# Four dense layers in exact fp32 on one core: first pieces and last pieces in halves, layer 1's small steps moved, and turned projections with one product for both halves of x

## The chip, the cores and the metric

One core of one Trainium2 chip. The metric is the device time of one execution in microseconds (us). The program holds all its work in one launch; its loops are unrolled when it is built.

## The reference, cut to what matters

x has 256 tokens of 2048 features and goes through four layers. Each is x + mix(rmsnorm(x) @ w_in) @ w_out, and a last rmsnorm follows:

```python
# layer 0: 8 heads of chunked attention with a relative bias, 4 heads of mLSTM       w_in 2048 x 9224
proj = rmsnorm(x, norm_g) @ w_in
y = concat(attention(qa, ka, va) * silu(za), sigmoid(ob) * mlstm(qb, kb, vb, gates) * silu(zb))
x = x + y @ w_out                                                                    # 2048 x 2048
# layer 1: RG-LRU behind a causal convolution, 8 heads of gated delta rule           w_in 2048 x 6160
# q, k, v: convolution, silu, l2norm of q and k; per head a 64-block triangular solve
# layer 2: 8 heads of a mixture of dilated windows, 4 heads of differential attention, rotary q and k
h = rmsnorm(x, norm_g) @ w_in                                                        # 2048 x 8192
yb = (softmax(q1 k1^T) - lam * softmax(q2 k2^T)) v
x = x + (concat(ya, yb) * silu(z)) @ w_out
# layer 3: 16 heads of causal attention, rotary q and k                              w_in 2048 x 8192
# out = rmsnorm(x) * final_norm
def _rope(t, pos):
    x1, x2 = split(t, 2, axis=-1)
    return t * cos + concat(-x2, x1) * sin
```

All is fp32.

## The kernel before, in words

**Products in three parts.** A product of fp32 matrices is made from fp32r parts: a = hi + lo, where hi is a copy in fp32r and lo what is left. ACC gets hi*hi + hi*lo + lo*hi. For x the parts are `XH` and `XL` (16 k-tiles of 128 features by 256 tokens), for a layer's output `YHA`, `YHB`, `YLA`, `YLB`; for the weights `WH` and `WL`.

**Jobs and pieces.** `job_list` (L77) names the projections in order; a job is 512 columns of a weight matrix (`few` jobs: 8 or 16). `piece_list` (L124) cuts each into pieces of 2 k-tiles x 512 columns (512 KB), 626 in all, and that order is the program's clock. For every piece SP issues a load into one of 8 `RAW` buffers (L600), ScalarE makes the high part (L985), VectorE the low one (L1330), and TensorE the products. `LOOK = 5`: the splits run five pieces ahead of the products; `WH` has 6 buffers. A load waits for the products eight pieces back.

**Two forms of product.** In "tok" form (L685 to 687) x is stationary and 512 columns of weights stream: 2 k-tiles x 2 token halves x 3 = 12 products per piece. In turned form ("feat", L692 to 694) 128 columns of weights are stationary and the 256 tokens stream: 2 x 4 x 3 = 24. Turned results stand feature by token, as scores need them. In layers 2 and 3 `q0`, `k0`, `q1`, `k1` are turned, two jobs each (b = 0, 1); the order there is q0 k0 v0 q1 k1 v1, then `zs`, `zg` and `out`.

**Accumulators.** Four PSUM banks `ACC0` to `ACC3`: job j uses two, and the first product of job j + 2 waits until job j is evacuated (L659 to 663). `evacuate` (L987 on ScalarE, L1332 on VectorE, L1821 on GpSimd) runs after a job's last piece. For a rotary job VectorE does, for each of two banks, one multiplication by cos (L1373) and two by sin on 64 partitions (L1377), and GpSimd adds them (L1849).

**The plan.** All other work is in small steps written out by hand. `put(slot, step, item, banks)` (L347) puts a step behind the products of piece `slot`; every engine walks the pieces and does its share of each step there (`go`), in order, so a step waits in its engine's queue behind all before it. PSUM banks `PM0` to `PM3` are dealt out in turn to steps that ask for them; a step waits until its bank was read (`read_out`). In `plan1` (L423), with b1 the first piece of layer 1: `norm_sum` (L845, 1200, 1622) sums the squares of q and k of four heads with 32 products of one column and takes two square roots; `delta_a`, `delta_k`, `delta_q` (L865 to 882) make the decayed products; `tri` (VectorE and ScalarE) inverts 16-blocks; `level_x` and `level_y` (L884, L900) join blocks at levels 4, 5 and 6, each using what ScalarE (L1242) or VectorE (L1697, L1701) made of the step before; `solve1` to `solve4`; `gate_lru`, `decay_lru`, `root_lru`, `scan` are the RG-LRU's. The functions of the scalar engine switch tables (ACT_TABLE_LOAD) between silu, square root, sigmoid and exponential.

**Start.** Transposed x lies in `Y` in six parts, and `x0` splits two k-tiles of it before each of the first eight pieces. `warm` (L697) issues 5 products on zeros before the first piece. A tile `VC` holds all per-partition vectors.

**End.** When the last job is added to x (L1362), ScalarE sums the last squares, `rms_a` makes 1/rms of both token halves, both engines scale what `gained` had multiplied by the final gain, and SP stores four times 512 columns of both halves (L637).

Of the kernel before, what the change touches and what calls it, by code (L numbers as in the profile page):

```python
# [14 lines left out]
D = 2048  # L15
# [6 lines left out]
WARM = 5  # L22
# [23 lines left out]
def constants():  # L46
# [13 lines left out]
    for window, dil in ((128, 1), (512, 4), (2048, 16)):  # L60
# [12 lines left out]
        "conv": (2, 0), "zc": (0, 2), "add": (0, 2), "rope": (0, 6)}  # L73
# [3 lines left out]
def job_list():  # L77
    jobs = []

    def both(layer, name, w, c0, mode, kind):  # L80
        for b in range(2):
            jobs.append(Job(layer, name, b, w, c0 + 512 * b, 512, mode, kind, (0, 1, 2, 3)))

# [28 lines left out]
    for layer, w, wo, at in ((2, "w_in_ab_2", "w_out_ab_2", ((3072, 4096, 5120, 7168), (0, 1024, 2048, 6144))),  # L112
                             (3, "w_in_c_2", "w_out_c_2", ((1024, 3072, 5120, 7168), (0, 2048, 4096, 6144)))):
        for n in range(2):
            both(layer, f"q{n}", w, at[n][0], "feat", "rope")
            both(layer, f"k{n}", w, at[n][1], "feat", "rope")
            both(layer, f"v{n}", w, at[n][2], "tok", "copy")
# [6 lines left out]
def piece_list(jobs):  # L124

    pieces = []
    for j, J in enumerate(jobs):
        if J.n < 128:
            pieces.append((j, 0, 16))
            continue  # L130
        pieces.extend((j, 4 * r + 2 * h, 2) for r in J.order for h in range(2))
# [6 lines left out]
def program(nc, I, out):  # L138
    ctx = ExitStack()
    with ctx:  # L140
# [14 lines left out]
        XH = sb("XH", KT * 256, F32R)  # L155
        XL = sb("XL", KT * 256, F32R)
# [15 lines left out]
        ACC = [ctx.enter_context(nc.psum_tensor(f"ACC{i}", [128, 512], F32)) for i in range(4)]  # L172
# [25 lines left out]
        XH3 = XH[:, :].rearrange("p (k c) -> p k c", k=KT)  # L198
        XL3 = XL[:, :].rearrange("p (k c) -> p k c", k=KT)
# [106 lines left out]
        ENDS[LAST[0] + 7] = ENDS.pop(LAST[0])  # L306
        A_AT = list(accumulate(EVAC[J.kind][0] for J in jobs))
        D_AT = list(accumulate(EVAC[J.kind][1] for J in jobs))
        GATE = [j for j, J in enumerate(jobs) if J.kind == "gate"]
# [43 lines left out]
        X_PARTS = ((0, 2), (2, 2), (4, 2), (6, 2), (8, 4), (12, 4))  # L353
# [69 lines left out]
        def plan1():  # L423
# [49 lines left out]
        def plan2(layer):  # L473
            b2 = F(layer, "q0", 0)
# [4 lines left out]
            if layer == 2:  # L479
                pairs_plan(L(2, "v0", 1) + 2)  # L480
            else:
                heads_plan(first, L(layer, "v0", 1) + 2, 4)
            heads_plan(first + 8, L(layer, "v1", 1) + 2, 4)
            if layer == 2:
                put(L(2, "v0", 1) + 44, "subln", 0)
                put(L(2, "v0", 1) + 45, "subln", 1)
# [26 lines left out]
        def around(p):  # L513
# [7 lines left out]
        s_xT = [sem(f"s_xT{i}") for i in range(len(X_PARTS))]  # L521
        s_raw = [sem(f"s_raw{i}") for i in range(NRAW)]
# [10 lines left out]
        s_rot, s_dsq, s_sub, s_sln, s_lmd, s_lma, s_gn, s_endD, s_endA = (  # L533
            sem(n) for n in ("s_rot", "s_dsq", "s_sub", "s_sln", "s_lmd", "s_lma", "s_gn", "s_endD", "s_endA"))
# [44 lines left out]
        def acc_of(j):  # L579
            return [ACC[2 * (j % 2)][:, :], ACC[2 * (j % 2) + 1][:, :]]  # L580

        x_rows = I["x"].rearrange("(t p) c -> p t c", p=128)
        n_cos, n_dil = COFF["cos"][0], COFF["dilated"][0]
# [5 lines left out]
        def sync(e):  # L589
# [3 lines left out]
            def load(p):  # L593
                j, k0, nk = pieces[p]
                J = jobs[j]
                dst = RAW[p % NRAW][:, 0:nk * J.n].rearrange("p (k n) -> p k n", k=nk)
# [1408 lines left out]
```

## Time and profile before

| what | us |
|---|---|
| median of 3 runs (lowest, highest) | 1950.43 (1948.64, 1951.62) |
| the profiled execution | 1949.87 |
| its span, first to last instruction | 1948.1 |
| TensorE busy | 1928.9 (99%) |
| VectorE busy | 1154.0 (59%) |
| ScalarE busy | 1011.4 (52%) |
| GpSimd busy | 150.8 (8%) |

PE is TensorE, DVE VectorE, ACT ScalarE, POOL GpSimd and SP the engine that issues the loads. PEld are loads of weights into TensorE, which run beside its products. The ends of matmuls are modelled; their starts are measured.

### The profile page before, as it was taken

What the parts mean: (1) busy time and instruction counts of PE and PEld (TensorE: products, weight loads), DVE (VectorE), ACT (ScalarE), POOL (GpSimd) and SP (SyncE); (2) the same over time, 40 slices, a digit from 0 to 9 for tenths busy, and PEclk for the clock granted to TensorE, in tenths of its full rate; (3) what the DMA queues carried; (4) which work ended last, traced back from release to release, by engine and by line L of the source; (5) the groups of instructions that cost most, each with busy time, mean ns of one, the idle gap of its engine ahead of it and who ended that gap; (6) DMA issues with size and microseconds to landing.
All of it is one profiled execution on the core that took longest, in us unless ns stands there. A gap on an engine that the chain in (4) does not pass through costs nothing.

```text
span 1948.1 us, 29186 instructions
## 1 busy us (share of the span) xinstructions
PE 1928.9 (99%) x11910; PEld 1730.3 (89%) x11910; DVE 1154.0 (59%) x1636; ACT 1011.4 (52%) x1571; POOL 150.8 (8%) x142
## 2 busy tenths in 40 slices
PE   9999999999999999999999999999999999999997
PEld 8988888888899999798899899888889989988886
DVE  6456554554656776687666566655566656654553
ACT  7344445664557655764543445456554344446643
POOL 0000000110001102100001001000000101100110
PEclk9999999999999989999999999999999999999999
DMA  9666566655564545444566655665556665565563
GB/s 331 176 182 179 161 188 181 174 167 186 184 169 149 163 120 143 150 147 157 184 188 184 192 172 162 182 179 163 174 183 179 183 190 166 159 186 173 160 205 119
DMA packets 178549, 340.45 MB, mean 175 GB/s; under 512 B 14592, under 2 KB 14848, under 8 KB 178288
## 3 DMA queue, kind: packets, MB, share of 16 engines
q1 hardware_dynamic: 177328, 334.81, 57.1%
q0 software_dynamic: 944, 3.61, 0.6%
q8 instruction: 95, 1.56, 0.3%
q14 instruction: 38, 0.31, 0.1%
q10 hardware_dynamic: 144, 0.16, 0.0%
HBM read 336.44 MB, written 2.10 MB: 174 GB/s over the span
## 4 chain that ended last, share of the span: by engine, by line
PE 92%; DVE 5%; ACT 2%; issue 1%; DVEq 0%; ACTq 0%
PE ACC L687 18%; PE ACC L685 18%; PE ACC L686 18%; PE ACC L692 11%; PE ACC L693 10%; PE ACC L694 10%; DVE WL L1330 2%; DVE S L1572 1%; ACT WH L985 1%; PE PM L774 1%; PE PM L789 1%; PE PM L827 1%; PE PM L811 1%; PE PM L812 1%; PE PM L810 1%
## 5 line engine op out<-in xcount | busy, mean ns | idle before, releaser
L1330 DVE TENSOR_TENSOR WL<-RAW,WH 128x1024 fp32r<-128x1024 f32 x624 | 779.0, 1262 | 611.4 <-ACT WH L985 609.5
L985 ACT ACTIVATE WH<-RAW 128x1024 fp32r<-128x1024 f32 x626 | 651.5, 1054 | 525.6 <-PE ACC L687 299.3
L692 PE MATMUL ACC<-XH,WH 128*128 128x256 f32 x1920 | 553.7, 288 | 0.0
L693 PE MATMUL ACC<-XL,WH 128*128 128x256 f32 x1920 | 546.3, 285 | 0.0
L694 PE MATMUL ACC<-XH,WL 128*128 128x256 f32 x1920 | 546.3, 285 | 0.0
L685 PE MATMUL ACC<-WH,XH 128*128 128x512 f32 x1024 | 407.1, 398 | 0.0
L687 PE MATMUL ACC<-WH,XL 128*128 128x512 f32 x1024 | 400.0, 391 | 0.0
L686 PE MATMUL ACC<-WL,XH 128*128 128x512 f32 x1024 | 399.6, 390 | 0.0
L692 PEld LDWEIGHTS ACC<-XH,WH 128*128 128x128 f32 x1920 | 371.1, 193 | 1.8 <-DVE WL L1330 0.4
L693 PEld LDWEIGHTS ACC<-XL,WH 128*128 128x128 f32 x1920 | 371.1, 193 | 1.0
L694 PEld LDWEIGHTS ACC<-XH,WL 128*128 128x128 f32 x1920 | 371.0, 193 | 0.0
L687 PEld LDWEIGHTS ACC<-WH,XL 128*128 128x128 f32 x1024 | 192.6, 188 | 40.5
L686 PEld LDWEIGHTS ACC<-WL,XH 128*128 128x128 f32 x1024 | 192.9, 188 | 39.1
L685 PEld LDWEIGHTS ACC<-WH,XH 128*128 128x128 f32 x1024 | 192.8, 188 | 39.0
L685 PE MATMUL ACC<-WH,YHB 128*128 128x512 f32 x256 | 101.0, 395 | 0.0
L685 PE MATMUL ACC<-WH,YHA 128*128 128x512 f32 x256 | 100.5, 393 | 0.0
L687 PE MATMUL ACC<-WH,YLB 128*128 128x512 f32 x256 | 99.9, 390 | 0.0
L687 PE MATMUL ACC<-WH,YLA 128*128 128x512 f32 x256 | 99.8, 390 | 0.0
L686 PE MATMUL ACC<-WL,YHB 128*128 128x512 f32 x256 | 99.7, 390 | 0.0
L686 PE MATMUL ACC<-WL,YHA 128*128 128x512 f32 x256 | 99.7, 389 | 0.0
L1849 POOL TENSOR_TENSOR S<-S 128x512 f32<-128x512 f32 x32 | 53.8, 1681 | 505.3 <-DVE S L1377 505.3
L687 PEld LDWEIGHTS ACC<-WH,YLB 128*128 128x128 f32 x256 | 48.1, 188 | 10.1
(336 smaller groups left out, 1613.1 us busy)
## 6 DMA issues: line engine op xcount, KB each, us to landing
RAW<-in_ev_w_in SPq DMA_DIRECT2D x144, 512.0 KB, 3.5
RAW<-in_w_in_ab SPq DMA_DIRECT2D x128, 512.0 KB, 3.6
RAW<-in_w_in_c SPq DMA_DIRECT2D x128, 512.0 KB, 3.6
RAW<-in_od_w_in SPq DMA_DIRECT2D x96, 512.0 KB, 3.7
RAW<-in_ev_w_out SPq DMA_DIRECT2D x32, 512.0 KB, 3.6
RAW<-in_od_w_out SPq DMA_DIRECT2D x32, 512.0 KB, 3.7
RAW<-in_w_out_ab SPq DMA_DIRECT2D x32, 512.0 KB, 3.7
RAW<-in_w_out_c SPq DMA_DIRECT2D x32, 512.0 KB, 3.8
```

The source lines that it names most:

```text
L685: e.matmul(o, th, hi[:, kk, :], start=f, stop=False)
L686: e.matmul(o, th, lo[:, kk, :], start=False, stop=False)
L687: m = e.matmul(o, tl, hi[:, kk, :], start=False, stop=l)
L692: e.matmul(o, wh, xh, start=f and g % 2 == 0, stop=False, skip_group_check=True)
L693: e.matmul(o, wh, xl, start=False, stop=False, skip_group_check=True)
L694: m = e.matmul(o, wl, xh, start=False, stop=l, skip_group_check=True)
L774: e.matmul(o[:, 128:384], qT[:, 128:256], kT, start=True, stop=True).then_inc(s_sc)
L789: m = e.transpose(o[:, c:c + 128], src[:, c:c + 128], ident)
L810: e.matmul(o[:, 0:dv], p[:, 0:128], v[0], start=True, stop=True)
L985: e.activation(hi, src, ACT.Copy).then_inc(s_hi)
L1330: e.tensor_tensor(lo, src, hi.bitcast(F32), ALU.subtract).then_inc(s_lo)
L1849: e.tensor_tensor(dst, dst, two(S6[:, 512 * i:512 * i + 512]), ALU.add).then_inc(s_rot)
```

## The change

1. **Wide form.** A new mode for the rotary projections of layers 2 and 3: jobs of 256 columns, pieces of 4 k-tiles x 256. `XH` and `XL` become one tile `XHL` in which the 256 high and the 256 low columns of a k-tile are neighbours, so one product of 512 columns gives hi*hi and hi*lo side by side in a bank, and a second one of 256 columns adds lo*hi to the left half. The evacuation first adds the halves (`tensor_reduce`), and then multiplies from SBUF; it empties ACC with that first operation. `ACC` is two tiles of two banks.
2. **Order.** `v0` comes before `q0` in layers 2 and 3; what hung on `v0`'s last piece hangs on the last of `k0`.
3. **Start.** `EARLY = 3`: the first three pieces are loaded, split and multiplied in halves of one k-tile (256 KB), the high products of a half before its low ones. The pieces of jobs 0 and 1 alternate. x comes in seven parts, the vectors in two DMAs. `WARM` is 4.
4. **End.** `TAIL = 4`: the last four pieces' products are done for the first token half, then for the second; each half is then added, normed, scaled and stored by itself, from ScalarE's queue (columns 0 to 1023) and SP's (1024 to 2047).
5. **Layer 1.** `norm_sum` in two steps of two heads in adjacent slots; level and solve steps of the first half one slot later (from level 5 on), all of the second half's one slot later, the RG-LRU's gates, decays and roots three slots later.
6. **Weights** lie packed in device memory, each piece as 128 rows of 4 KB in a row, where a piece was 2 x 128 rows of 2 KB.

```diff
-WARM = 5
+TAIL = 4
+WARM = 4
+EARLY = 3
...
-        "conv": (2, 0), "zc": (0, 2), "add": (0, 2), "rope": (0, 6)}
+        "conv": (2, 0), "zc": (0, 2), "add": (0, 2), "rope": (0, 4)}
...
+    def wide(layer, name, w, c0, kind):
+        for i in range(4):
+            jobs.append(Job(layer, name, i, w, c0 + 256 * i, 256, "wide", kind, (0, 1, 2, 3)))
...
+            if n == 0:
+                both(layer, "v0", w, at[0][2], "tok", "copy")
+            wide(layer, f"q{n}", w, at[n][0], "rope")
+            wide(layer, f"k{n}", w, at[n][1], "rope")
+            if n == 1:
+                both(layer, "v1", w, at[1][2], "tok", "copy")
...
+        if j == 1:
+            pieces[:] = [p for both in zip(pieces[:8], pieces[8:]) for p in both]
...
                 put(b1 + at[0], "norm_sq", half)
-                put(b1 + at[1], "norm_sum", half, 1)
+                for i in range(2):
+                        put(b1 + at[1] + i, "norm_sum", (half, i), 1)
...
-                    (0, (24, 25), (26, 28, 30, 32, 34), (36, 37, 38, 39, 40, 42, 44, 45, 46, 47), (50, 52, 53, 55, 56, 58),
-                     (60, 61, 62, 63, 64), (85, 87, 89)),
-                    (1, (64, 65), (66, 68, 70, 71, 72), tuple(range(73, 83)), (85, 87, 89, 91, 93, 95), (97, 99, 101, 103, 104),
+                    (0, (24, 25), (26, 28, 30, 32, 34), (36, 37, 38, 39, 40, 42, 44, 45, 46, 47), (50, 52, 54, 56, 57, 59),
+                     (61, 62, 63, 64, 65), (85, 87, 89)),
+                    (1, (65, 66), (67, 69, 71, 72, 73), tuple(range(74, 84)), (86, 88, 90, 92, 94, 96), (98, 100, 102, 103, 104),
                      (105, 105, 107))):
...
-                put(b1 + 71 + n // 2, "gate_lru", n, 1)
-                put(b1 + 75 + n // 2, "decay_lru", n)
-                put(b1 + 79 + n // 4, "root_lru", n)
-                put(b1 + (81, 83, 84, 86, 90, 92, 94, 95)[n], "scan", n)
+                put(b1 + 74 + n // 2, "gate_lru", n, 1)
+                put(b1 + 78 + n // 2, "decay_lru", n)
+                put(b1 + 82 + n // 4, "root_lru", n)
+                put(b1 + (84, 85, 86, 87, 90, 92, 94, 95)[n], "scan", n)
...
+                    elif J.mode == "wide":
+                        for g in range(2):
+                            wh, wl = hi[:, kk, 128 * g:128 * g + 128], lo[:, kk, 128 * g:128 * g + 128]
+                            e.matmul(acc[g], wh, XHL3[:, kt, :], start=f, stop=False)
+                            m = e.matmul(acc[g][:, 0:256], wl, xh, start=False, stop=l)
+                    elif p < EARLY:
+                        e.wait_ge((s_hi0, s_hi)[kk], p + 1)
+                        for g in range(4):
...
+            def last_products():
+                for t in range(2):
+                    for p in range(NP - TAIL, NP):
...
+                        if t == 0:
+                            e.wait_ge(s_lo, p + 1)
...
+                        if t:
+                            m.then_inc(s_mm)
+                    if t == 0:
+                        m.then_inc(s_half)
...
                     e.wait_ge(s_mm, p + 1)
+                    e.tensor_reduce(dst, halves_of(j), AX, ALU.add).then_inc(s_evD)
                     e.wait_ge(s_row, J.layer + 1)
-                    for i in range(2):
-                        ps, dst = two(acc[i]), feat(s)[:, 4 * J.b + 2 * i:4 * J.b + 2 * i + 2, :]
-                        t2 = two(S6[:, 512 * i:512 * i + 512])
-                        e.tensor_tensor(dst, ps, cos, ALU.mult).then_inc(s_evD)
-                        if r:
-                            e.wait_ge(s_rot, 2 * r - 1 + i)
-                        for x, y in ((lo, hi), (hi, lo)):
-                            e.tensor_tensor(t2[x], ps[y], sin[y], ALU.mult).then_inc(s_evD)
+                    if r > 1:
+                        e.wait_ge(s_rot, r - 1)
+                    e.wait_ge(s_evD, D_AT[j] - 3)
+                    for x, y in ((lo, hi), (hi, lo)):
+                        e.tensor_tensor(t2[x], dst[y], sin[y], ALU.mult).then_inc(s_evD)
+                    e.wait_ge(s_evD, D_AT[j] - 1)
+                    e.tensor_tensor(dst, dst, cos, ALU.mult).then_inc(s_evD)
```

## Rows read from the trace of the kernel before

**Rows 1.** The page: busy us (share) and instructions; granted clock by fortieth of the span.
```profile
PE 1928.9 (99%) x11910; PEld 1730.3 (89%) x11910; DVE 1154.0 (59%) x1636; ACT 1011.4 (52%) x1571; POOL 150.8 (8%) x142
PEclk9999999999999989999999999999999999999999
```
**Rows 2.** TensorE's waits: who waited for what, us in total, times, longest.
```profile
PE PM L895 <- DVE SC L1701: 2.9, 2, 2.1
PE PM L953 <- DVE S L1652: 2.1, 1, 2.1
...
PE PM L895 <- issue: 1.4, 1, 1.4
```
**Rows 3.** Windows of `k0`, `v0` and `k1` (with attention), layer 2: busy us by engine.
```profile
1028.85:1074.93 46.08, 46.08 (x386) 46.08 (x385) 29.73 (x28) 16.97 (x16) 7.26 (x4) 1.00 0.63 184
1074.93:1118.48 43.55, 43.55 (x194) 36.06 (x193) 25.42 (x23) 17.54 (x17) 3.64 (x2) 1.00 0.65 192
...
1167.46:1219.38 51.92, 51.92 (x420) 51.40 (x419) 35.80 (x50) 25.06 (x50) 5.16 (x4) 1.00 0.54 163
```
**Rows 4.** The page's costliest groups: busy us, mean ns, idle before, releaser.
```profile
L1330 DVE TENSOR_TENSOR WL<-RAW,WH 128x1024 fp32r<-128x1024 f32 x624 | 779.0, 1262 | 611.4 <-ACT WH L985 609.5
L985 ACT ACTIVATE WH<-RAW 128x1024 fp32r<-128x1024 f32 x626 | 651.5, 1054 | 525.6 <-PE ACC L687 299.3
L692 PE MATMUL ACC<-XH,WH 128*128 128x256 f32 x1920 | 553.7, 288 | 0.0
```
**Rows 5.** Timelines of the start, TensorE and VectorE: start us, us, instruction.
```profile
7.06 0.59 PE L701 MATMUL PM<-S 128*128 128x512 f32 x1
...
7.92 0.59 PE L701 MATMUL PM<-S 128*128 128x512 f32 x1
8.06 0.56 PE L692 MATMUL ACC<-XH,WH 128*128 128x256 f32 x1
...
6.78 1.23 DVE L1330 TENSOR_TENSOR WL<-RAW,WH 128x1024 fp32r<-128x1024 f32 x1 [0.37 <-ACT WH L985]
```
**Rows 6.** Timeline of the end, and the stores' line with time to landing.
```profile
1936.86 0.39 PE L687 MATMUL ACC<-WH,YLA 128*128 128x512 f32 x1
1937.29 1.29 DVE L1362 TENSOR_TENSOR X<-ACC,X 128x512 f32<-128x512 f32 x2 [13.69 <-PE ACC L687]
...
1940.10 0.17 DVE L1400 RECIPROCAL SM<-SM 128x2 f32<-128x2 f32 x1 [0.36 <-ACT SM L1078]
1940.30 1.95 ACT L1322 ACTIVATE Y<-Y,SM 128x512 f32<-128x512 f32 x3 [0.23 <-DVE SM L1400]
...
1941.50 1.41 DVE L1816 SCALAR_TENSOR_TENSOR Y<-X,SM,S 128x512 f32<-128x512 f32 x2
...
L637 SPq DMA_DIRECT2D out<-Y x4: 384/440/1075, 1941.1 to 1942.9; - x4
...
DMA to landing us min/median/max: 2.8/3.8/4.7
```
**Rows 7.** Windows of layer 1 behind three of its small steps; granted clock third from last.
```profile
613.80:617.40 3.60, 3.60 (x20) 3.60 (x20) 3.04 (x8) 3.43 (x6) 3.60 (x6) 0.54 0.00 0
...
721.20:726.60 5.40, 5.40 (x29) 5.40 (x26) 1.73 (x2) 1.59 (x3) 0.00 (x0) 0.50 0.01 3
794.40:798.20 3.80, 3.80 (x12) 2.92 (x12) 0.26 (x2) 3.47 (x8) 0.31 (x1) 0.58 0.00 0
```
**Rows 8.** Timelines of layer 1: TensorE at the first `norm_sum`, ScalarE around the second.
```profile
610.29 3.63 PE L852 MATMUL PM<-C,S 128*128 128x1 f32 x32
...
701.90 1.28 ACT L1200 ACT_TABLE_LOAD   x1
...
709.89 1.06 ACT L1242 ACTIVATE SC<-PM 128x512 f32<-128x512 f32 x2
```
**Rows 9.** VectorE's groups kept apart by shape: busy us, mean ns, idle before.
```profile
L1377 DVE TENSOR_TENSOR S<-ACC,C 64x512 f32<-64x512 f32 x64 | 44.0, 688 | 2.0
...
L1513 DVE TENSOR_REDUCE SM<-SC 128x1 f32<-128x256 f32 x40 | 16.3, 409 | 0.0
```

More of the change, by code:

```diff
@@ L130, in piece_list @@
             continue
+        if J.mode == "wide":
+            pieces.extend((j, 4 * r, 4) for r in J.order)
+            continue
         pieces.extend((j, 4 * r + 2 * h, 2) for r in J.order for h in range(2))
+        if j == 1:
+            pieces[:] = [p for both in zip(pieces[:8], pieces[8:]) for p in both]
         if J.name == "out" and J.b == 1:
@@ L305, in program @@
         ENDS = {p: (j,) for j, p in LAST.items()}
-        ENDS[LAST[0] + 7] = ENDS.pop(LAST[0])
+        del ENDS[NP - 1]
         A_AT = list(accumulate(EVAC[J.kind][0] for J in jobs))
         D_AT = list(accumulate(EVAC[J.kind][1] for J in jobs))
+        FEW = [j for j, J in enumerate(jobs) if J.kind == "few"]
         GATE = [j for j, J in enumerate(jobs) if J.kind == "gate"]
@@ L473, in plan2 @@
         def plan2(layer):
-            b2 = F(layer, "q0", 0)
+            b2 = F(layer, "v0", 0)
             if layer == 2:
@@ L594, in load @@
                 j, k0, nk = pieces[p]
-                J = jobs[j]
-                dst = RAW[p % NRAW][:, 0:nk * J.n].rearrange("p (k n) -> p k n", k=nk)
-                src = I[J.w].rearrange("(k p) n -> p k n", p=128)[:, k0:k0 + nk, J.c0:J.c0 + J.n]
+                dst = RAW[p % NRAW][:, 0:nk * jobs[j].n]
+                src = I[f"few{jobs[j].layer}"] if nk == 16 else I["w"][p - sum(FIRST[f] < p for f in FEW)]
+                if p < EARLY:
+                    e.dma_start(dst[:, 0:512], src[:, 0:512]).then_inc(s_raw0[p], 16)
+                    if p == 0:
+                        load_xT(1)
+                    dst, src = dst[:, 512:1024], src[:, 512:1024]
                 if p >= NRAW:
@@ L695, in products @@
                 m.then_inc(s_mm)
+            def last_products():
+                assert all(step not in steps for p in range(NP - TAIL, NP) for x in around(p) for step, _, _ in x)
+                for t in range(2):
+                    for p in range(NP - TAIL, NP):
+                        j, k0, nk = pieces[p]
+                        hi, lo = (x[:, :].rearrange("p (k n) -> p k n", k=nk) for x in (WH[p % NHL], WL[p % NRAW]))
+                        o = acc_of(j)[t]
+                        if t == 0:
+                            e.wait_ge(s_lo, p + 1)
+                        for kk in range(nk):
+                            kt = k0 + kk
+                            th, tl = (x[kt // 8][:, kt % 8, 128 * t:128 * t + 128] for x in (YH8, YL8))
+                            e.matmul(o, th, hi[:, kk, :], start=False, stop=False)
+                            e.matmul(o, th, lo[:, kk, :], start=False, stop=False)
+                            m = e.matmul(o, tl, hi[:, kk, :], start=False, stop=p == NP - 1 and kk == nk - 1)
+                        if t:
+                            m.then_inc(s_mm)
+                    if t == 0:
+                        m.then_inc(s_half)
             def warm(_, b):
@@ L843, in decays3, with norm_sum @@
                 read_out[b] = (s_dd, 11)
-            def norm_sum(half, b):
+            def norm_sum(item, b):
+                half, part = item
                 e.wait_ge(s_nsq, half + 1)
                 o = bank(b)
-                for j in range(4):
+                for j in (2 * part, 2 * part + 1):
                     for i in range(2):
@@ L854, in norm_sum @@
                 m.then_inc(s_nt)
-                read_out[b] = (s_na, 2 * half + 2)
+                read_out[b] = (s_na, 4 * half + 2 * part + 2)
             def turn_v(h, b):
@@ L968, in tensor @@
             go(plan[-1])
-            for p in range(NP):
+            for p in range(NP - TAIL):
                 before, after = around(p)
@@ L1620, in decays3, with norm_sum @@
                 e.tensor_scalar(sp4, sp4, -4.0, None, ALU.mult).then_inc(s_dd)
-            def norm_sum(half, b):
+            def norm_sum(item, b):
+                half, part = item
+                if part == 0:
+                    return
                 hs = slice(4 * half, 4 * half + 4)
-                e.wait_ge(s_na, 2 * half + 1)
+                e.wait_ge(s_na, 4 * half + 3)
                 e.reciprocal(rq[:, :, hs], rq[:, :, hs]).then_inc(s_nr)
@@ L1957, in col @@
         return v.reshape(-1, 128).T
-    m = {n: _np.ascontiguousarray(a[n][0]) for n in BIG}
+    m, packed = {}, []
+    jobs = job_list()
+    for j, k0, nk in piece_list(jobs):
+        J = jobs[j]
+        x = a[J.w][0][128 * k0:128 * (k0 + nk), J.c0:J.c0 + J.n]
+        x = _np.ascontiguousarray(x.reshape(nk, 128, J.n).transpose(1, 0, 2).reshape(128, nk * J.n))
+        if nk == 16:
+            m[f"few{J.layer}"] = x
+        else:
+            packed.append(x)
+    m["w"] = _np.stack(packed)
     m["x"] = _np.ascontiguousarray(a["x"][0])
```

186 lines of the change are left out of this document (113 added, 73 removed).

## The prediction

> **What bounds the kernel now.** I read the busy times first. TensorE is busy 99% of the span and its granted clock is full in nearly every slice [rows 1]; VectorE and ScalarE stand at 59% and 52%. The list of TensorE's waits comes next: it holds some 6 us of waiting in all, and everything of size in it lies in layer 1's small steps [rows 2]. So the length of the program is the number of product instructions times their spacing, plus the start, the tail and a few places in layer 1. The end of a matmul in the trace is modelled (288 ns for 256 columns, [rows 4]), and these instructions start closer together than that, so I take no duration from it but divide windows. Sixteen pieces of `k0` in layer 2 (24 products of 256 columns each) take 46.08 us, 2.880 us a piece, 0.120 us a product. Sixteen pieces of `v0` (12 products of 512 columns) take 43.55 us, 2.722 a piece, 0.2268 a product [rows 3]. The 256 added columns cost 0.1068 us, so a product carries 0.013 us beside its columns. Each piece costs ScalarE 1.05 us and VectorE 1.26 us for its two parts [rows 4], under half of either spacing, five pieces ahead. The loads are covered by a ring of 8 pieces (22 us).
>
> **The wide projections.** Eight names (`q0 k0 q1 k1` in layers 2 and 3) of 1024 columns over 16 k-tiles are 1024 tiles of weights, of the 1920 in turned form [rows 4]. Each took three 256-column products, 3 x 0.120 = 0.360 us; it now takes one of 512 columns and one of 256, 0.2268 + 0.120 = 0.3468. Per piece of 8 tiles that is 2.774 against 2.880; 128 pieces x 0.106 = 13.5 us, all on the bounding engine. No row shows the two forms alternating. Bounds: nothing, if the alternation costs the spacing of a product, and 27 us, if the short product hides its own 0.013 behind the long one as well (another 1024 x 0.013). I take 13.5, since both forms have rows of their own.
> The Trainium skill ("TensorE: Matmul & The Clock Gate", the section on 56 ns against 53.3 ns) puts only about 2.5 ns beside the columns of a matmul. By that the merged product would bring 1024 x 2.5 ns = 2.6 us, not 13.5. The trace speaks against it here (13 ns), but it is a rival below.
>
> What hangs on the wide form: VectorE now adds the two halves first. That `tensor_reduce` of 1024 elements has no row; a reduce of 256 took 0.41 us and an element-wise operation on 512 took 0.69 [rows 9]. Its bounds are 1.1 and 1.7 us; I take 1.4. With three operations at 0.69 a job's evacuation is 3.5 us, every 4 pieces (11.1 us), where it was 4.1 us every 8. VectorE in the busiest stretch, `k1` with attention, was busy 35.8 of 51.9 us [rows 3]; it gets 4 x 3.5 - 2 x 4.1 = 5.8 more in about 50: 83%. GpSimd's rotary additions stay 32. The accumulators are to be emptied in 11 us, not 23: about 4 us are needed. So nothing on the path. `v0` put ahead of `q0` makes its first pieces 0.16 us shorter; the transposed x it needs is made in the second slot of the layer and used in the seventh: nothing. GpSimd's mask and lambda DMAs move with it; their readers come 50 pieces later. The load of the tables behind SP's wait comes 16 pieces after `k1`, as before.
>
> **The start.** The first product starts behind the warm-up, whose eighth record starts at 7.06 and tenth at 7.92; VectorE's first low part ended at 8.01 [rows 5]. With four warm-up products for five the path is free two records earlier, 0.86 us. Then the data must be there by 7.5: ScalarE's part of the first half needs about 0.6 us behind a landing that is no later than before, VectorE's another 0.6; with the 6.78 of rows 5 for the whole tile, half of it is ready by 6.9. Interleaving jobs 0 and 1 halves the x asked for. SP issues four more DMAs and ScalarE's queue one more; all are parts of those of before, and bring the first bytes forward. Taken 0.9 (bounds: -1.5, if a half lands late behind the extra issues, and 1.5).
>
> **The tail.** The last product starts at 1936.86 and takes 0.39; the span is 1948.1, so 10.85 us lie behind it [rows 1, 6]. Up to the reciprocal's end (1940.27) both token halves are in the chain, 3.0 us; one half alone saves an add or square of 0.8: 2.2. Then ScalarE copies two of 0.65 (now 3 in 1.95) or VectorE does two of at most 0.70 (half of its 1.41 there): 2.2 + 1.3 = 3.5 us. The four stores, first issued at 1941.1 and the last at 1942.9 landing 4.7 later, take 6.5 us together, and one alone 2.8 [rows 6], so each further one 1.24. Two at the end are 4.0, plus the 0.5 from the last landing to the end: 8.0. That saves 2.85. The first half's chain starts 24 products (5.4 us) before the end and its stores are out by then; a clash with them would cost up to 1.2. Bounds 1.5 and 3.5.
>
> **Layer 1.** Three kinds of place:
> - `norm_sum`: 32 one-column products take 3.6 us [rows 8], and behind both of them the clock is at 0.54 for 3.6 us [rows 7] (one of two alike is shown): 0.46 x 3.6 = 1.66 each, 3.3. In halves with a piece between, I expect no drop; two more switches into the small products are put at 0.2 each, an estimate without a row: gain 2.9 (bounds -0.5 and 2.9). The price is on ScalarE: the square roots are now in two slots with a silu step between, so one pair of table loads more, 1.28 each [rows 8].
> - The first half's `level_x` waited 2.9 us for VectorE's subtractions of L1701 [rows 2], and the clock stood at 0.50 for 5.4 us behind it [rows 7]: 5.6 in all. One piece later (2.9) covers the wait. But level 4's copies on ScalarE start at 709.9 [rows 8], just as `level_y` asks for them, and the two table loads (2.6 us) come before; TensorE arrives 0.8 us earlier as well. I let `level_y` wait 2.3 in its place: gain 3.3 (bounds -1 and 5.6).
> - `gate_lru` waited 2.1 for a bank that the delta step of the same slot held [rows 2], and the clock at 0.58 for 3.8 us [rows 7] took 1.6. Three slots later it is behind the last delta step: gain 3.7 (bounds 1 and 3.7).
> - The second `level_x`, 1.4 without a named releaser [rows 2]: its triangular steps are now ahead of the scans, but `decay_lru` now shares a slot with `zd`'s silu (one table load more), and four scans and the evacuation of `zc` lie before level 4's subtractions. Taken at nothing (bounds -3 and 1.4).
> Sum 9.9; the bounds together -3.5 and 13.6.
>
> **The sum.** 13.5 + 0.9 + 2.85 + 9.9 = 27.2 us. Against the profiled execution's 1949.87 (span 1948.1 and 1.8 around it) that is 1922.7; the median of the runs is 0.56 above it: 1923 us.
>
> **Rivals.**
> 1. Layer 1 gives nothing: ScalarE's added table loads and the shifted steps make as many waits as went. For it: ScalarE and VectorE wait for each other there, and I only followed two places. Against: two waits have a plain cause that the move takes away. 1949.9 - 17.3 = 1932.6, so 1933.
> 2. The fixed part of a product isn't saved (the three products' 0.360 is the spacing of their loads of weights, or the skill's 2.5 ns holds): 2.6 of 13.5 comes, 1934. Against: 0.120 and 0.2268 hold over 16 pieces each.
> 3. All but the wide products comes at its lower bound: 13.5 - 1.5 + 1.5 - 3.5 = 10.0, so 1940.
> 4. Slower: VectorE doesn't empty the wide jobs in time. Place: the first product of each of 32 jobs, which waits for the evacuation of the job before the last. Four pieces give 11.1 us, in `k1` 12.5 (a quarter of 51.9, less the saving); low parts take 4 x 1.26 = 5.0 and attention 1.9 (a quarter of 35.8 - 16 x 1.26 - 8.2), so an evacuation above 5.6 us makes VectorE the bound. To eat 27 us it must be over by 0.85 per job, a reduce of 6.45 - 2.1 = 4.4; at 5.0 it would be 32 x 1.5 = 48 of loss, 1971 beside the forecast. Rows 9 put the reduce at a third of that.
>
> **Chances.** Forecast (1916 to 1929) 0.65; rival 1 0.15; rival 2 0.07; rival 3 0.05; rival 4 0.04; better than 1916, 0.04. The range 1914 to 1935 holds the first three cases and part of the last, and leaves some 0.12 out: rivals 3 and 4 and what is better than 1914. A difference of 0.2% (3.9 us) is about what can be told from none. Faster 0.94, within it 0.02, slower 0.04.
>
> **What would show it.** Wide pieces at 2.77 us each in a window, 2.88 if the fixed part stays. The first 256-column product at about 7.6 us. Eight us between the last product and the end. In layer 1: no half clock behind `norm_sum`; no wait at `gate_lru`; a wait of about 2 us at the first `level_y` instead of the `level_x` after it. VectorE near 80% in `k1`. I am wrong if TensorE waits at the starts of wide jobs, or if the clock still falls in layer 1 in four places.

## The result, and the profile after

The changed kernel takes 1936.74 us in the median of 4 runs (1935.91 to 1937.08), the kernel before beside it 1950.25 (1948.64 to 1951.62). The ratio is 0.9928, with a 95% interval of 0.9916 to 0.9939: 13.5 us faster, where 27 were forecast. The profiled execution took 1936.95, its span is 1935.2.

The page's busy line, and TensorE's waits in the changed kernel (us in total, times, longest), against [rows 1, 2]:

```profile
PE 1919.3 (99%) x10884; PEld 1673.8 (86%) x10884; DVE 1204.1 (62%) x1672; ACT 1017.6 (53%) x1583; POOL 165.1 (9%) x142
```
```profile
PE PM L890 <- DVE SC L1796: 3.8, 1, 3.8
PE PM L916 <- ACT S L1267: 2.3, 1, 2.3
PE PM L764 <- DVE S L1477: 1.5, 1, 1.5
PE PM L959 <- issue: 0.2, 1, 0.2
```

The three waits of [rows 2] are gone. Two of the same size stand in their place: L916 is the second half's `norm_sum`, which waits for ScalarE's squares, and L890 is `ty` (the transposes of the normed output). L764 is only the warm-up.

The same windows as in [rows 3, 7], of the changed kernel: `k0` and `k1` of layer 2; the stretch behind the first part of the first `norm_sum`; behind the second half's `norm_sum`; around level 4; behind `ty`. The clock is third from last.

```profile
1068.54:1113.77 45.23, 45.23 (x258) 39.24 (x257) 36.25 (x32) 16.97 (x16) 8.81 (x4) 1.00 0.57 186
1161.82:1212.48 50.66, 50.66 (x292) 44.38 (x291) 42.99 (x55) 24.95 (x50) 6.98 (x4) 1.00 0.51 167
...
611.20:614.80 3.60, 3.60 (x33) 3.60 (x32) 1.70 (x2) 3.57 (x7) 3.60 (x3) 1.00 0.32 118
692.90:699.30 6.40, 6.40 (x32) 6.40 (x32) 6.05 (x19) 2.33 (x5) 0.00 (x0) 0.50 0.01 4
711.00:716.00 5.00, 5.00 (x47) 5.00 (x45) 4.10 (x8) 4.50 (x7) 0.00 (x0) 1.00 0.58 195
...
855.00:860.00 5.00, 5.00 (x25) 5.00 (x24) 3.63 (x5) 4.15 (x5) 0.79 (x1) 0.50 0.00 0
```

The reader is to see three things. Sixteen wide pieces take 45.23 us, 2.827 each, not 2.774. The first `norm_sum` and level 4 run at the full clock now. But behind each of the two new waits the clock is halved, for 6.8 and 5.9 us (the windows above show 6.4 and 5.0 of them).

TensorE's lead over the kernel before, from the starts of the same piece in both traces, tells where the 13 us come from:

| at the start of | lead, us | this stretch | forecast |
|---|---|---|---|
| the first products (spacing full) | 0.80 | +0.80 | +0.9 |
| layer 1, slot b1+27 | 2.30 | +1.50 | +1.45 (first `norm_sum`) |
| slot b1+51 | -1.80 | -4.10 | +1.45 (second `norm_sum`) |
| slot b1+80 | 8.44 | +10.24 | +7.0 (first `level_x`, `gate_lru`) |
| slot b1+104 | 3.08 | -5.36 | 0 (second `level_x`) |
| layer 2 | 3.10 | +0.02 | 0 |
| last product | 10.16 | +7.06 | +13.5 (wide products) |
| end of the span | 12.9 | +2.76 | +2.85 (tail) |

Start and end of the changed kernel, its timelines (start us, us, instruction), against [rows 5, 6]:

```profile
1.46 6.33 PE L764 MATMUL PM<-S 128*128 128x512 f32 x8 [1.46 <-DVE S L1477]
7.22 0.68 PE L724 MATMUL ACC<-XHL,WH 128*128 128x256 f32 x1
...
1926.70 0.39 PE L754 MATMUL ACC<-WH,YLA 128*128 128x512 f32 x1
...
1929.32 1.33 ACT L1406 ACTIVATE Y<-Y,SM 128x512 f32<-128x512 f32 x2 [0.23 <-DVE SM L1917]
1930.68 0.35 ACTq L1408 DMA_DIRECT2D out<-Y  x1
```

From the last product's start to the end of the span it is 8.5 us, against 1948.1 - 1936.86 = 11.24 before.

The first row hangs on the start, which differs from execution to execution by more than 1 us (last section). Packed weights and the new order (parts 6 and 2) have no experiment of their own; no wait for a load stands in either list of TensorE's waits, and the lead stays at 0.80 through layer 0 and at 3.1 from slot b1+104 to layer 2.

### The profile page after: what moved, and what is told of

Read it like the earlier page. It is cut to its first block, busy times and chain, and to the rows that moved or that the text cites. A ratio compares the mean times of both kernels' runs of the same rounds, so it can differ in the third digit from the quotient of the medians.

```text
span 1935.2 us, 27225 instructions
## 1 busy us (share of the span) xinstructions
PE 1919.3 (99%) x10884; PEld 1673.8 (86%) x10884; DVE 1204.1 (62%) x1672; ACT 1017.6 (53%) x1583; POOL 165.1 (9%) x142
## 4 chain that ended last, share of the span: by engine, by line
PE 93%; DVE 3%; ACT 3%; issue 1%; ACTq 0%
PE ACC L711 18%; PE ACC L713 18%; PE ACC L712 18%; PE ACC L717 12%; PE ACC L718 6%; PE ACC L734 4%; PE ACC L735 4%; PE ACC L736 4%; DVE WL L1426 1%; ACT WH L1061 1%; PE PM L837 1%; PE PM L890 1%; DVE S L1668 1%; PE PM L852 1%; PE PM L874 1%
## 5 line engine op out<-in xcount | busy, mean ns | idle before, releaser
L1426 DVE TENSOR_TENSOR WL<-RAW,WH 128x1024 fp32r<-128x1024 f32 (+1 forms) x624 | 794.2, 1288 | 560.9 <-ACT WH L1061 559.9
L1061 ACT ACTIVATE WH<-RAW 128x1024 fp32r<-128x1024 f32 (+1 forms) x626 | 649.8, 1052 | 517.5 <-PE ACC L713 286.2
L711 PE MATMUL ACC<-WH,XHL 128*128 128x512 f32 x1024 | 407.2, 398 | 0.0
L713 PE MATMUL ACC<-WH,XHL 128*128 128x512 f32 x1024 | 399.1, 390 | 0.0
L712 PE MATMUL ACC<-WL,XHL 128*128 128x512 f32 x1024 | 398.7, 389 | 0.0
L717 PE MATMUL ACC<-XHL,WH 128*128 128x512 f32 x1024 | 365.0, 401 | 0.0
L718 PE MATMUL ACC<-XHL,WL 128*128 128x256 f32 x1024 | 287.3, 281 | 0.0
L734 PE MATMUL ACC<-XHL,WH 128*128 128x256 f32 x872 | 251.8, 289 | 0.0
L735 PE MATMUL ACC<-XHL,WH 128*128 128x256 f32 x872 | 248.2, 285 | 0.0
L736 PE MATMUL ACC<-XHL,WL 128*128 128x256 f32 x872 | 248.2, 285 | 0.0
L717 PEld LDWEIGHTS ACC<-XHL,WH 128*128 128x128 f32 x1024 | 192.4, 188 | 47.2
L713 PEld LDWEIGHTS ACC<-WH,XHL 128*128 128x128 f32 x1024 | 192.2, 188 | 40.7
L711 PEld LDWEIGHTS ACC<-WH,XHL 128*128 128x128 f32 x1024 | 192.4, 188 | 38.8
L718 PEld LDWEIGHTS ACC<-XHL,WL 128*128 128x128 f32 x1024 | 193.4, 189 | 0.5
L734 PEld LDWEIGHTS ACC<-XHL,WH 128*128 128x128 f32 x872 | 169.1, 194 | 0.6
L735 PEld LDWEIGHTS ACC<-XHL,WH 128*128 128x128 f32 x872 | 169.0, 194 | 0.2
L736 PEld LDWEIGHTS ACC<-XHL,WL 128*128 128x128 f32 x872 | 168.8, 194 | 0.0
```

The lines of the kernel that those rows point to most:

```text
L711: e.matmul(o, th, hi[:, kk, :], start=f, stop=False)
L712: e.matmul(o, th, lo[:, kk, :], start=False, stop=False)
L713: m = e.matmul(o, tl, hi[:, kk, :], start=False, stop=l)
L717: e.matmul(acc[g], wh, XHL3[:, kt, :], start=f, stop=False)
L718: m = e.matmul(acc[g][:, 0:256], wl, xh, start=False, stop=l)
L734: e.matmul(o, wh, xh, start=f and g % 2 == 0, stop=False, skip_group_check=True)
```

## The experiments

Each time is the median of four executions, with the kernel before beside it, whose medians there were 1949.2 to 1950.5 on four chips. Differences are told against the changed kernel's 1936.7; told by the lead over the kernel beside it they shift by 0.3 us at most, but for the last run. Unless said otherwise an experiment is the changed kernel with the edit shown. The edits are shortened; `long` and `short` stand for the product of 512 and that of 256 columns.

### The products of the wide form

**k_three_short**: the long product cut in two again.

```diff
-e.matmul(acc[g], wh, XHL3[:, kt, :], start=f, stop=False)
+e.matmul(acc[g][:, 0:256], wh, xh, start=f, stop=False)
+e.matmul(acc[g][:, 256:512], wh, xl, start=False, stop=l)
```

> The changed kernel with the long product of the wide form cut back into its two short ones (hi*hi and hi*lo, 256 columns each, into the two halves of the bank); jobs, order, evacuation and all else kept. It measures the merging alone. Theory 1 (merging is worth 0.360 - 0.353 per weight tile, what the trace shows): a wide piece takes 2.88 us for 2.82, 128 x 0.056 = 7.1 us more than the changed kernel, about 1943.9. The prediction's term was 13.5 us; the rule of a 2.5 ns fixed part would give 2.6 us.

Measured: 1942.73 us (1941.83 to 1943.96), 6.0 more, where 7.1 were expected. **d_long_first**: the eight long products of a piece, then the eight short ones.

```diff
-for kk in range(nk): for g in range(2): long(kk, g); short(kk, g)
+for kk in range(nk): for g in range(2): long(kk, g)
+for kk in range(nk): for g in range(2): short(kk, g)
```

> The changed kernel with the products of a wide piece in another order: its eight products of 512 columns first, then its eight of 256. Same products, banks and weights. In the changed kernel a 512-column product and the 256-column one behind it start 0.236 and 0.117 us apart from their followers, 0.353 together, where 0.2268 + 0.120 = 0.3468 was predicted. Theory 1 (the step from a long product to a short one costs about 6 ns net): one such step per piece for eight, a piece takes 2.78 us for 2.824, 128 x 0.045 = 5.8 us less. Theory 2 (a product of both halves of x costs more than one of 512 weight columns, whatever follows): no change, pieces stay at 2.82.

Measured: 1932.95 us (1932.38 to 1933.45), 3.8 less, where 5.8 were expected. **c_other_bank**: long and short in turns, each short one into the other bank.

```diff
+long(0,0), then for each k: long(k,1), short(k,0), long(k+1,0), short(k,1)
```

> The changed kernel with long and short products of a wide piece still taking turns, but each short one going to the other PSUM bank than the long one ahead of it. Theory 1 (long to short costs, whatever the bank): a piece stays at 2.82, no change (seven such steps for eight, under 1 us). Theory 3 (a short product that adds to the bank that the long one ahead of it still writes costs the 6 ns): a piece takes 2.78, about 5 us less.

Measured: 1935.72 us (1935.01 to 1936.52), 1.0 less. The same window, 16 pieces of `k0` in layer 2, in these three, in this order:

```profile
1068.78:1114.86 46.08, 46.08 (x386) 46.08 (x385) 36.46 (x32) 17.00 (x16) 8.85 (x4) 1.00 0.53 183
```
```profile
1068.18:1112.88 44.70, 44.70 (x259) 39.33 (x258) 36.06 (x32) 17.00 (x16) 8.81 (x4) 1.00 0.58 188
```
```profile
1069.08:1114.20 45.12, 45.12 (x259) 39.22 (x257) 36.19 (x32) 16.98 (x16) 8.84 (x4) 1.00 0.57 188
```

Three short ones take 46.08, to the hundredth what the kernel before took; in turns 45.23; long first 44.70; 44.38 was forecast (16 x 2.774). So merging saves 6.6 ns per weight tile (0.85 us over 128 tiles) in the order of the change and 10.8 with long first, of the 13.2 forecast. That a short product follows a long one into its bank is not the reason: with that changed, 0.11 of the missing 0.85 came back, and that run has seven such steps a piece for eight. (It puts the long product behind the short one into the same bank instead; but in the turned form of the kernel before neighbours share a bank too, three in a row, and their spacing is 0.120.) That long and short ones take turns is most of it, as grouping them gives 0.53 of the 0.85 back. A stretch of the changed kernel's products:

```profile
1080.08 0.28 PE L718 MATMUL ACC<-XHL,WL 128*128 128x256 f32 x1
1080.20 0.40 PE L717 MATMUL ACC<-XHL,WH 128*128 128x512 f32 x1
1080.44 0.28 PE L718 MATMUL ACC<-XHL,WL 128*128 128x256 f32 x1
```

A pair starts every 0.36 or 0.35 us. Over more than 100 pieces the medians are 0.236 from long to short and 0.117 from short to long: 0.353, where 0.2268 + 0.120 = 0.3468 had been added up. With long first, the medians of the eight long products are 233, 236, 228, 233, 231, 227, 227, 227 ns: the extra cost comes in the first five behind the short ones and then is gone; seven short ones take 119 or 120 and the first 113. What in the engine makes it isn't shown.

### Layer 1

**g_layer1_old**: all of part 5 undone (slots and `norm_sum` as in the kernel before), the other parts kept.

```diff
-put(b1 + at[1] + i, "norm_sum", (half, i), 1)
+put(b1 + at[1], "norm_sum", (half, i), 1)
...
-put(b1 + 74 + n // 2, "gate_lru", n, 1)
+put(b1 + 71 + n // 2, "gate_lru", n, 1)
...
```

> The changed kernel with part 5 undone: norm_sum whole, and the levels, solves, gates, decays, roots and scans of layer 1 in the slots of the kernel before; all other parts kept. Theory 1 (the parts add up: start 0.8, wide products 7.1, tail 2.75, layer 1 about 1.5 of 9.9): 1.5 us more than the changed kernel, about 1938.2, with the old waits back at the first level_x and gate_lru and no wait at norm_sum. Theory 2 (layer 1 as predicted, 9.9, and the loss lies elsewhere): 1946.

Measured: 1938.00 us (1937.78 to 1938.59), 1.3 more. Part 5 as a whole is worth 1.3 us in these runs, not 9.9. The time is the expected one, but not the way to it: theory 1 said that there is no wait at `norm_sum`, and there is one.

```profile
PE PM L916 <- ACT S L1267: 1.3, 1, 1.3
```

What makes it is seen beside the next run. **f_sum_whole**: only `norm_sum` put back in one slot, by the first line of that diff.

> The changed kernel with both parts of each norm_sum back in one slot (b1+24, and b1+48), all else kept. Theory 1 (the split costs ScalarE a second pair of table loads, 1.28 us each, so its squares of the second half come 0.2 us later than before while TensorE comes 2.3 us earlier; wait and half clock there are made by the split itself): the half clock behind the first norm_sum comes back (1.5 us more), the 2.3 us wait and 1.5 of half clock at the second go; TensorE reaches slot 51 at about 704.1 us for 706.6, in all 1 to 2.6 us less than the changed kernel. Theory 2 (the split is a gain of some 3 us as predicted and the wait has another source): 1.5 to 3 us more.

Measured: 1933.31 us (1932.77 to 1937.25), 3.4 less: the split, forecast as a gain of 2.9, is a loss of that size. (Three of its four executions lie within 0.8 us; the fourth, 1937.25, stands 3.7 above them.) By the two traces 1.5 us are lost again at the first one (the half clock behind 32 products in a row) and 4.1 won at the second. The reason is on ScalarE. Its timelines, first of the changed kernel around the first `norm_sum` and at the second half's squares (L1267), then of this one at the squares:

```profile
610.79 1.28 ACT L1276 ACT_TABLE_LOAD   x1
612.08 0.27 ACT L1276 ACTIVATE SM<-PM,VC 128x4 f32<-128x4 f32 x1
...
614.26 1.28 ACT L1242 ACT_TABLE_LOAD   x1
617.79 0.95 ACT L1242 ACTIVATE S<-S 128x256 f32<-128x256 f32 x2 [2.25 <-DVE S L1668]
618.76 1.28 ACT L1276 ACT_TABLE_LOAD   x1
620.06 0.27 ACT L1276 ACTIVATE SM<-PM,VC 128x4 f32<-128x4 f32 x1
...
621.44 1.28 ACT L1289 ACT_TABLE_LOAD   x1
...
689.83 2.54 ACT L1267 ACTIVATE S<-S 128x256 f32<-128x256 f32 x8
```
```profile
688.46 2.55 ACT L1267 ACTIVATE S<-S 128x256 f32<-128x256 f32 x8
```

In the kernel before the squares ran from 689.62 and TensorE asked for them at 692.25, just as they ended: no wait stood in the list, and no slack was there either. ScalarE and VectorE alternate through the convolutions and keep their own pace from the first `norm_sum` on. The second pair of roots with its table load at 618.76 puts ScalarE 0.2 us later than before although it had begun 0.8 earlier, and TensorE arrives 2.3 earlier: it waits 2.3 and then runs 6.8 us at half clock. All that had been gained up to there is paid back, and 1.8 more. Counted from the first product, the squares begin at 681.6 to 681.8 us in the five traces with `norm_sum` whole and at 682.5 to 683.0 in the nine with it split: about 1 us is the price of the split on ScalarE.

The rest of the wait is TensorE's own lead, and g_layer1_old shows it alone. Up to slot b1+50 it is the same program as f_sum_whole, and yet behind the first `norm_sum` the clock fell in this one and not in g_layer1_old; the same window of the two:

```profile
613.50:617.00 3.50, 3.50 (x19) 3.50 (x18) 3.43 (x9) 2.70 (x4) 3.50 (x7) 0.51 0.00 0
```
```profile
613.50:617.00 3.50, 3.50 (x30) 3.50 (x31) 3.07 (x8) 3.44 (x6) 3.50 (x6) 1.00 0.00 0
```

Of the five traces with the first `norm_sum` whole it fell in four; in the nine with it split it fell in none, as forecast. The 1.5 us that g_layer1_old saved there by luck it paid at the squares, which come no earlier for it: 1.3 of waiting, then 6.8 at half clock, and at b1+51 it stood 1.7 us behind f_sum_whole (each counted from its first product). So its 1.3 us for all of part 5 is no firmer than about 1.7, and f_sum_whole's slow fourth execution may be one of this kind; no trace of it shows that.

**h_roots_once**: TensorE's sums stay split, ScalarE takes the roots of both parts in the second one (one pair of loads).

```diff
+if part == 0:
+    return
+e.wait_ge(s_nt, 2 * half + 2)
+for part in (0, 1): (the two square roots of that part)
```

> The changed kernel with ScalarE taking all the square roots of a half in the second norm_sum step (one pair of table loads for two); TensorE's sums stay split. Theory 1 (ScalarE's chain sets TensorE's time from the first norm_sum to level_y in slot 52): ScalarE runs 1.4 us earlier or more, the wait for its squares falls from 2.3 to about 0.8 us and the half clock behind it shrinks; 1.5 to 3 us less by slot 53. Theory 2 (VectorE's convolution and tri steps set it, the table loads are hidden): no change, the 2.3 us wait stays.

Measured: 1935.43 us (1935.22 to 1935.74), 1.3 less, and the wait for the squares is still 2.2, as theory 2 has it. In this execution the first product began 0.88 earlier than in the changed kernel's, and slot b1+49 began 2.26 earlier. That isn't the table load: a_ty91 (below), the changed kernel's own code up to slot b1+88, also began 0.88 earlier and reached b1+49 2.13 earlier. In these two traces the clock was halved behind the wait for 3.4 us only, where it was 6.8 in the changed kernel's. Two stretches behind the wait, here:

```profile
694.50:697.90 3.40, 3.40 (x19) 3.40 (x17) 3.26 (x9) 0.59 (x2) 0.00 (x0) 0.50 0.00 0
697.90:701.30 3.40, 3.40 (x31) 3.40 (x31) 2.17 (x5) 3.33 (x7) 0.57 (x1) 1.00 0.47 154
```

Between a_ty91 and this run lie 0.1 us at the squares and 0.2 by slot b1+53. So the load that this edit takes away, the one at 610.79, is hidden: behind the silu load that follows it ScalarE waits 2.3 us for VectorE anyway. The load between the convolution and the exponential (618.76 above) stands here too, at 617.50, and the squares are as late as in the other split versions. What the 1.3 us of the medians come from isn't shown. **e_sum49**: the second half's sums one slot later.

```diff
-(1, (45, 48, 57, 59))
+(1, (45, 49, 57, 59))
```

> The changed kernel with the second half's two norm_sum steps one slot later (b1+49 and 50 for 48 and 49). In the changed kernel TensorE waits 2.3 us there for ScalarE's squares and the clock is halved for 6.4 us behind the wait. Theory 1 (ScalarE's chain since the first norm_sum runs at its own pace, 0.2 us later than before, while TensorE arrives 2.3 us earlier, so one piece more covers the wait): wait and half clock go, 2.5 + 3.2 = 5.7 us less at slot 51, of which later waits may take part; total 4 to 5.7 us less. Theory 2 (ScalarE's and VectorE's work in slots 50 to 58 is the limit and TensorE only waits elsewhere): under 1.5 us less, with a new wait at a delta or tri step.

Measured: 1936.96 us (1936.00 to 1937.82), no change: theory 2, though the new wait is at a level step and not at a delta or `tri` step. The waits:

```profile
PE PM L973 <- ACT SC L1318: 4.1, 1, 4.1
PE PM L890 <- DVE SC L1796: 3.8, 1, 3.8
```

The wait at `norm_sum` is gone, and 4.1 us stand at `level_y` of level 4 (L973), whose copies (L1318) are behind both table loads and four roots in ScalarE's queue. At slot b1+50 TensorE was 7.6 us ahead of the changed kernel, at b1+53 it was 0.6 behind. A wait that is moved over without giving the engine waited for less to do comes back at the next step that needs it.

**a_ty91**: the first half's `ty` from slot b1+89 to 91.

```diff
-(61, 62, 63, 64, 65), (85, 87, 89)),
+(61, 62, 63, 64, 65), (85, 87, 91)),
```

> The changed kernel with one step moved: the transposes of the first half's normed output (`ty`, two of them) from slot b1+89 to b1+91. In the changed kernel TensorE waits 3.8 us in slot 89 for VectorE's level-4 subtractions, and the clock is halved for 5 us behind it. Theory 1 (the wait is for a PSUM bank: level_y moved from 87 to 88 took all four banks one slot ahead of `ty`): the wait and the half clock go, 5.4 us less, about 1931.4. Theory 2 (VectorE itself is behind there, its scans, splits and the evacuation of zc fill 836 to 857): the next step that needs VectorE, level_x of level 5 in slot 90, waits 2 to 4 us in its place, gain under 2 us.

Measured: 1933.57 us (1931.82 to 1934.40), 3.2 less. Its waits:

```profile
PE PM L916 <- ACT S L1267: 2.3, 1, 2.3
PE PM L959 <- DVE SC L1800: 2.2, 2, 1.4
```

Beyond the 0.88 us that it had from its start, the gain at slot b1+90 is 5.6, as theory 1 has it. At b1+92 1.4 of it are left: the next level (L959, `level_x`) waits 2.2 in two parts, as theory 2 has it, and the clock falls behind these waits all the same (0.50 from 854.9 to 861.7 us). That is less than the 3.2 of the medians; the kept trace is the slowest of the four executions. The cause of the wait is the ring of PSUM banks: level 4's `level_y`, moved from 87 to 88, takes all four, and `ty` in 89 needs one. VectorE reads them late, since it is full: in the changed kernel its level 4 subtractions come behind scans, splits and the evacuation of `zc`:

```profile
850.78 0.69 DVE L1846 TENSOR_TENSOR_SCAN Y<-S 128x256 f32<-128x256 f32 x1
851.39 1.20 DVE L1426 TENSOR_TENSOR WL<-RAW,WH 128x1024 fp32r<-128x1024 f32 x1
852.51 1.28 DVE L1454 TENSOR_TENSOR S<-ACC,C 128x512 f32<-128x512 f32 x2
853.71 0.68 DVE L1796 TENSOR_TENSOR SC<-SC,PM 128x512 f32<-128x512 f32 x1
```

### Versions that beat both

**i_combo**: long first, roots once, the second half's sums at 49 and 50, the first half's level 4 `level_y` at 53, `ty` at 90, the second half's levels from 5 on one slot later.

```diff
-(50, 52, 54, 56, 57, 59)    (86, 88, 90, 92, 94, 96)    (85, 87, 89)
+(50, 53, 55, 57, 58, 60)    (86, 88, 91, 93, 95, 97)    (85, 87, 90)
```

> A better version, from what the runs so far point to: wide pieces with the eight long products first; roots taken once per half; the second half's sums at b1+49 and 50; the first half's level_y of level 4 at 53 and its later levels one slot later; `ty` of the first half at 90; the second half's levels from 5 on one slot later (91, 93, 95, 97). If the waits for ScalarE and VectorE are covered: long first 3.8 less, slots 85 to 92 up to 5.4 less, slots 48 to 53 up to 5 less: 1936.7 - 3.8 - 4.5 - 4 = about 1924.5. If TensorE only meets ScalarE or VectorE elsewhere: 1929 to 1931.

Measured: 1927.45 us (1926.31 to 1927.72), between the two. It has its waits in small pieces, 4.4 us at the steps of the levels, and the granted clock is 1.00 from 600 to 900 us. **l_combo_whole**: the same `ty`, later levels of the second half, and long first; but `norm_sum` whole and the first half's levels as in the change.

> Another way to the better version: long products first, norm_sum whole in slots b1+24 and b1+48, `ty` at 90, second half's levels from 5 on at 91, 93, 95, 97; the rest as in the changed kernel. The parts measured alone: whole sums -3.4, long first -3.8, ty and later levels -3 to -5: 1924.5 to 1926.5, against 1927.5 of the version with the roots taken once. Rival (VectorE is full from 836 to 857 and again takes what TensorE gains): 1928 or more.

Measured: 1925.22 us (1924.95 to 1927.05), as expected. Its list of waits, behind the warm-up's line:

```profile
PE PM L903 <- DVE SC L1809: 1.0, 1, 1.0
PE PM L972 <- issue: 0.2, 1, 0.2
```

**n_combo_warm2** is i_combo with two warm-up products for four (`WARM = 2`), and **o_best** is l_combo_whole with the same.

> The version with long first, roots once and moved slots (1927.5), with two warm-up products for four. In the profiled executions of one and the same start code the first product began between 6.10 and 7.59 us, always right behind the warm-up, whose 8 records take 0.43 us each at the full clock and 0.85 at half, while the first half's data is ready at 5.4 to 5.6. Theory 1 (the warm-up is the path, and products at half clock do useful work in its place): first product at 5.5 us, 0.5 to 1.5 us less. Theory 2 (the clock rises later with fewer warm-up products or with a gap between them and the first product): products stay at half clock beyond 7 us, equal or up to 2 us more.

> The version with norm_sum whole (1925.2) and two warm-up products for four. Theory 1 (the start and layer 1 add up; in the two profiled executions with two and four warm-up products the first one began its first product 0.55 us earlier and had 0.65 to 0.9 us left of it after the first pieces): 1924.4, with the first product at 5.5 us. Theory 2 (what is gained at the start meets the same wait of TensorE in layer 1 or the difference is within the spread of the start): 1925.2, no change.

Measured: 1926.76 us (1925.84 to 1927.22) against 1927.45, and 1924.71 (1923.94 to 1925.69) against 1925.22, on other chips. The first products of n_combo_warm2:

```profile
1.46 3.78 PE L777 MATMUL PM<-S 128*128 128x512 f32 x4 [1.46 <-DVE S L1495]
5.55 0.36 PE L737 MATMUL ACC<-XHL,WH 128*128 128x256 f32 x1 [0.31 <-ACT WH L1066]
5.74 0.28 PE L738 MATMUL ACC<-XHL,WH 128*128 128x256 f32 x1
```

They start at 5.55 as data allows, and 0.12 us apart from the second on; theory 2's slow products don't come. The two differences of 0.7 and 0.5 us are no more than the runs' own spread, and against the kernel before beside each, o_best is no faster than l_combo_whole: ratio 0.9874 (0.9857 to 0.9890) and 0.9873 (0.9858 to 0.9887). A gain in time from the shorter warm-up isn't shown, and these two are the fastest versions measured.

## Why the prediction was wrong

Of 27.2 us 13.5 came. Three terms failed: the wide products were mis-sized by 6.4 us, and two steps of layer 1 that were put at a gain of 1.45 and at nothing lost 4.1 and 5.4.

**Wide products (13.5 forecast, 7.1 came): the mechanism right, the term mis-sized.** The step that failed is "I take 13.5, since both forms have rows of their own". Rows of two pure sequences gave the spacing of each form, and the sum was made as if they were additive in a mixture. The bound of that step had named the alternation; it costs 6.2 ns a pair (0.353 for 0.3468), 1024 x 6.2 ns = 6.3 us, which is the difference. Rival 2, by which only 2.6 us come, is refuted too: three short ones put back cost 6.0 us. The Trainium skill ("TensorE: Matmul & The Clock Gate", the section on 56 ns against 53.3 ns) gives some 2.5 ns for a product's fixed part; merging saved 6.6 ns here, and 10.8 in the better order, so the runs agree neither with it nor with the 13 of the sum.

**Rest of the wide form: right.** The added reduce took 1.22 us (forecast 1.4; its line stands below), VectorE stood at 43.0 of 50.7 us in `k1`, 85% (83%), and no wait at a wide job is in the list. Rival 4 never came near.

```profile
L1466 DVE TENSOR_REDUCE S<-ACC 128x512 f32<-128x1024 f32 x32 | 39.1, 1223 | 9.1 <-PE ACC L718 8.9
```

**Start and tail: right**, 0.8 and 2.76 for 0.9 and 2.85. The start's number is less firm than the agreement suggests (below).

**Layer 1 (9.9 forecast, 2.3 by the traces, 1.3 by undoing it): two of its steps failed.** Rival 1 had the mechanism, that as many waits are made as go; its 1933 us supposed the whole 13.5 of the wide products.
- First `level_x` and `gate_lru`, 7.0 forecast, 10.2 came. The 2.3 us that I let `level_y` wait did not appear, for a bad reason: TensorE came to it 1.8 us later than before, where I had it come 0.8 earlier. Where it came earlier, the wait stood there: 1.0 us in a_ty91 (at 711.22), 4.1 in e_sum49.
- Second `norm_sum`, +1.45 forecast, -4.1 came. The failed step is "The price is on ScalarE: [...] one pair of table loads more, 1.28 each". It was named and then put at nothing in the sum, without a reason. But its squares ended in the same moment in which TensorE asked for them (692.17 and 692.25 us), so the microsecond that ScalarE lost and each that TensorE gained ahead of this place were waited for. The same holds for the gain of 1.45 at the first `norm_sum`: the clock stayed up there, as forecast, and TensorE only came to the squares earlier, as g_layer1_old shows. The slack of the next step that meets the other engine wasn't looked up.
- Second `level_x`, 0 forecast, -5.4 came, outside the bound of -3. I had asked what the moved levels wait for, and not who stands behind them in the ring of PSUM banks. `ty`, which wasn't moved, did: 3.8 us and some 2.9 of half clock, less the 1.4 that `level_x` itself had waited before. The prediction had seen exactly this kind of wait at `gate_lru`.

Both new waits also cost what they did to the clock: 0.50 for 6.8 and 5.9 us behind them, some 3.4 and 2.9 us of products. A wait of 2.3 us that is not covered was a loss of 5.7, against which only the 1.7 stand that the kernel before had lost there to its own half clock: 4.0, and the table has 4.1.

The forecast's 27.2 minus 6.4 (wide) minus 5.5 and 5.4 (the two new waits) plus 3.2 (first levels and `gate_lru`) is 13.1, against 12.9 in the spans.

## What to carry to other kernels

A fine plan around a full engine gains only up to the next step at which that engine meets another: before counting a gain, look up at each such step when the other engine was done and when the full one asked, and where the two times agree, the gain ends there. Before reading a difference of 1 or 2 us out of two profiles, look at where the first product began and at how long the clock was halved behind each wait in both: the same code differed by that much here. Count who asks for a bank, a buffer or a queue next behind each moved step, above all the steps that stay where they are. And where two forms of an instruction are to alternate, their spacings in pure sequences don't give the price of the mixture; measure it, and try each form in a group.

## What the runs showed of the hardware

- In the turned products, long (512 columns) and short ones (256) in turns start 0.236 and 0.117 us apart, 6.2 ns more a pair than in pure sequences; grouped by eight, the cost falls to 2.5 ns a pair (44.70 for 44.38 us over 128 pairs). Sending the short product to another PSUM bank than the long one ahead of it gave back no more than 0.11 us in 16 pieces.
- What an uncovered wait does to TensorE's clock differs between executions of the same code. Behind the wait of 2.2 to 2.4 us at the second `norm_sum` the granted clock was 0.50 for 6.8 us in four traces and for 3.4 in two; behind 32 products of one column in a row it fell for 3.4 us in four traces and not in the fifth.
- With one and the same start code, the first product began between 6.10 and 7.65 us in the eleven profiled executions with four warm-up products, each time right behind the warm-up. The warm-up's records stand 0.853 us apart at first and 0.430 later, and what differs is how many of them are slow; the granted clock in the profile stands at 1.00 all the while. So 1.5 us of difference between two profiles of this program can be the start alone, and 0.8 of the change's lead is no firmer than that. What decides it isn't shown here. The Trainium skill ("TensorE: Matmul & The Clock Gate", "What's actually happening") says of the number of slow products at the start that it varies from run to run with one and the same kernel, and these eleven agree with that.
